# Two token batches in a transformer step: the first three tiles run ahead, and their expert rows are gathered beside the second batch

## The reference

```python
xn = rms_norm(x, norm_mix_g)
dq, dk, dv, sq, sk, sv, ga, gb = project_in(xn, w_in, pos)        # 4352 columns, RoPE on q and k
oa = diff_attn(dq, dk, dv, lam)       # 4 heads, two softmaxes each, causal by chunks of 64
ob = swa(sq, sk, sv, sinks)           # 8 heads, window of 128 tokens
h = x + (ga * (rms(oa) @ w_a) + gb * (ob @ w_b)) @ w_out
h = h + mem_attn(rms_norm(h, norm_mem_g), mk, mv, w_mem_q, w_mem_o)   # 256 memory tokens
# PEER: 128 x 128 experts of one neuron, 8 heads, each takes the best 16
q = rms_norm(h) @ w_peer_q;  s1, s2 = q1 @ keys1, q2 @ keys2
idx, g = top 16 of v1[i] + v2[j], softmax of their scores
h = h + sum over the 8 * 16 chosen of gelu(xn . u[idx]) * g * v[idx]
y = rms_norm(h, final_norm_g)
```

## Time and profile before

| | us |
|---|---|
| median of 3 runs | 4893.45 (4890.81 to 4926.24) |
| the profiled execution | 4913.51 |
| its span in the trace | 4911.7 |

### The profile page before, as it was taken

The page is one execution under the profiler, slowest core; times in us unless marked ns, Lnnn a source line. Parts: engine busy times, 40 slices in busy tenths (PEclk is TensorE's granted clock), DMA queues, the critical chain, the costliest instruction groups (busy, mean ns, idle before and its releaser), DMA issues. The chain is left out here.

```text
span 4911.7 us, 61601 instructions
## 1 busy us (share of the span) xinstructions
PE 4164.9 (85%) x20219; PEld 3480.8 (71%) x20219; DVE 3159.5 (64%) x5709; ACT 1297.4 (26%) x2699; POOL 626.9 (13%) x505
## 2 busy tenths in 40 slices
PE   6999798998887875355552699999999999999996
PEld 5788556786444665344442599999999999999996
DVE  4301333111111217999998599999999999999896
ACT  3111222111111211144443222222232223222222
POOL 0000000000000000033333111111111111111110
PEclk9999667555999977688887799999999999999998
DMA  4322320102014010022223777777777777777774
GB/s 139 112 90 77 86 65 17 41 19 86 26 34 154 0 39 5 5 73 73 73 73 96 269 278 284 285 274 281 276 287 278 277 279 274 280 276 278 273 273 173
DMA packets 323883, 770.86 MB, mean 157 GB/s; under 512 B 29120, under 2 KB 170944, under 8 KB 274112
## 3 DMA queue, kind: packets, MB, share of 16 engines
q1 hardware_dynamic: 248992, 356.77, 22.2%
q0 software_dynamic: 55360, 403.60, 21.7%
q10 hardware_dynamic: 19440, 9.44, 0.7%
HBM read 681.01 MB, written 89.78 MB: 157 GB/s over the span
## 5 line engine op out<-in xcount | busy, mean ns | idle before, releaser
L2078 PE MATMUL exp_h<-exp_xh,exp_uh 128*128 128x384 f32 x2048 | 688.8, 336 | 59.6 <-DVE exp_xl L2048 56.4
L2080 PE MATMUL exp_h<-exp_xh,exp_ul 128*128 128x384 f32 x2048 | 688.2, 336 | 0.0
L2079 PE MATMUL exp_h<-exp_xl,exp_uh 128*128 128x384 f32 x2048 | 687.4, 336 | 0.0
L1900 POOL DMA_INDIRECT exp_uv<-in_peer_uv,gidx x384 | 373.8, 973 | 1783.6 <-DVE H L2010 1735.9
L2092 PE MATMUL exp_y<-exp_vh,exp_ah 128*128 128x512 f32 x1536 | 598.2, 389 | 3.3 <-DVE H L1983 3.3
L2094 PE MATMUL exp_y<-exp_vh,exp_al 128*128 128x512 f32 x1536 | 600.6, 391 | 0.0
L2093 PE MATMUL exp_y<-exp_vl,exp_ah 128*128 128x512 f32 x1536 | 600.3, 391 | 0.0
L2004 DVE SCALAR_TENSOR_TENSOR exp_uv<-exp_uv,exp_gx 128x1024 f32<-128x1024 f32 x384 | 469.0, 1222 | 62.4 <-DMA exp_uv<-in_peer_uv,gidx 39.1
L2010 DVE SCALAR_TENSOR_TENSOR H<-exp_uv,exp_coef,H 128x1024 f32<-128x1024 f32 x384 | 491.2, 1280 | 24.0 <-ACT exp_coef L1945 24.0
L1983 DVE TENSOR_TENSOR H<-H,exp_y 128x512 f32<-128x512 f32 x768 | 490.3, 679 | 3.8 <-PE exp_y L2094 3.6
L2078 PEld LDWEIGHTS exp_h<-exp_xh,exp_uh 128*128 128x128 f32 x2048 | 386.5, 189 | 66.2 <-issue 53.6
(11 more groups left out here) (276 smaller groups left out, 6327.6 us busy)
## 6 DMA issues: line engine op xcount, KB each, us to landing
exp_u<-in_peer_u SPq DMA_DIRECT2D x128, 512.0 KB, 4.8
exp_v<-in_peer_v SPq DMA_DIRECT2D x128, 512.0 KB, 4.0
s_w<-top_tile_w SPq DMA_DIRECT2D x6, 8192.0 KB, 30.4
exp_w<-s_w SPq DMA_DIRECT2D x128, 384.0 KB, 3.0
out_z<-proj_zs SPq DMA_DIRECT2D x72, 256.0 KB, 2.0
proj_w<-in_w_in SPq DMA_DIRECT2D x16, 1024.0 KB, 5.4
merge_gates<-out_z SPq DMA_DIRECT2D x9, 1024.0 KB, 5.0
s_zt<-proj_zt ACTq DMA_DIRECT2D x27, 256.0 KB, 2.3
```

The source lines that it names most:

```text
L1900: pool.indirect_dma_start(out=uv[j][:, :], out_offset=None, in_=I["peer_uv"], in_offset=bass.IndirectOffsetOnAxis(ap=K["gidx"][:, e, j:j + ...
L2078: pe.matmul(hp[c][:, 0:TC], uh[s][:, n, :], xh[:, n, at], start=(n == 0), stop=False)
L2079: pe.matmul(hp[c][:, 0:TC], uh[s][:, n, :], xl[:, n, at], start=False, stop=False)
L2080: last = pe.matmul(hp[c][:, 0:TC], ul[s][:, n, :], xh[:, n, at], start=False, stop=(n == KD - 1))
```

## The change

- The tiles are two batches. Batch A is tiles 0 to 2, and it runs projection, both attentions, merge, memory and retrieval first. Batch B is tiles 3 to 8, and it then runs the same stages. The experts and final stages follow once for all. Every stage's weights are loaded (and, in the projection, split) in both batches. B's attention reads k and v of all tiles.
- All of A's three tiles are gathered; of B's six, two are gathered (`NG = 2`) and four dense (`ND = 4`). The output half of a dense tile is a piece; of the eight pieces five (`HELD`) stay in PSUM over all 128 steps, and three take turns in one bank `turned`, which DVE empties by `add_turn`.
- A's gathers are single rows of 4 KB (512 KB for 128 tokens): 384 of u, then 384 of v. The first 640 of them (all u, and v of tiles 0 and 1) are taken inside B's stages, by numbers in the code (`rows.take`): 110 in projection, 154 in differential attention, 120 in window attention, 120 in merge, 136 in memory. They come through a ring of four buffers (`RING`). The last 128 (v of tile 2) are taken in the experts stage, one a step (`add_early`). Two small stages are new, `phase_rows` (scales A's tiles) and `phase_coefficients` (the gelu of A's dot products).
- B's gathered tiles have two buffers each instead of one.
- In `choose` a reduction over 16 is written as four additions. Most counted loops of the first stages are unrolled.

```diff
-NG = 3
-ND = NT - NG
+NA = 3
+NG = 2
+ND = NT - NA - NG
 MD = ND * P
+RING = 4
...
+NROW = 128
+QUOTA = {"project": 110, "diff": 264, "window": 384, "merge": 504, "memory": 640}
+NU = NA * NROW
+NV_FRONT = 2 * NROW
...
+    def fetch(self, pool, stage):
+
+        K = self.K
+        end = RING if stage is None else min(QUOTA[stage] + RING, QUOTA["memory"])
+        for n in range(self.fetched, end):
+            tile, e = self.choice(n)
+            if n >= RING:
+                pool.wait_ge(K["row_used"], n - RING + 1)
+            pool.indirect_dma_start(out=K["row"][n % RING][:, :], out_offset=None,
+                                    in_=self.I["peer_u_rows"] if n < NU else self.I["peer_v_rows"],
+                                    in_offset=bass.IndirectOffsetOnAxis(ap=K["gidx"][:, e, tile:tile + 1], axis=0))\
+                .then_inc(K["row_in"][n % RING], 16)
+        self.fetched = end
...
+    def take(self, dve, count):
+        K = self.K
+        for n in range(self.taken, self.taken + count):
+            tile, e = self.choice(n)
+            row = K["row"][n % RING]
+            if n >= NU and n % 2 == 0:
+                dve.drain()
+            dve.wait_ge(K["row_in"][n % RING], 16 * (n // RING + 1))
+            if n < NU:
+                dve.scalar_tensor_tensor(out=row[:, :], in0=row[:, :], scalar=1.0, in1=K["gx"][:, tile, :],
+                                         op0=ALU.mult, op1=ALU.mult, accum_out=K["hs"][:, tile, e:e + 1]).then_inc(K["row_used"], 1)
+            else:
+                dve.scalar_tensor_tensor(out=K["H"][:, tile, :], in0=row[:, :], scalar=K["coef"][:, tile, e:e + 1],
+                                         in1=K["H"][:, tile, :], op0=ALU.mult, op1=ALU.add).then_inc(K["row_used"], 1)
+        self.taken += count
...
-        arrive = [0, 1, 2, 2, 3, 3, 4, 4, 4]
+        arrive = [0, 1, 2, 2, 3, 3][:NT]
...
-                        if t in (3, 7):
-                            low_w(c + 1, t // 7)
-                with dve.Fori(ROPED, ROPED + PLAIN - 1) as c:
+                        if rows:
+                            rows.take(dve, 2)
+                        if t in (early + 1, min(late + 1, NT - 1)):
+                            low_w(c + 1, int(t > early + 1))
+                for c in range(ROPED, ROPED + PLAIN - 1):
                     for half in range(2):
                         low_w(c + 1, half)
+                        if rows:
+                            rows.take(dve, 9)
...
                             combine(*at(pair, x - 1))
+                            if rows:
+                                rows.take(dve, 2)
...
-                with dve.Fori(1, NT - 1) as t:
+                for t in range(1, NT - 1):
+                    if rows:
+                        rows.take(dve, 9)
                     dve.drain()
                     merged(t, False)
                     normed(t + 1)
+                    if rows:
+                        rows.take(dve, 9)
                     residual(t - 1)
+                if rows:
...
-                        dve.tensor_reduce(picked[:, a, :], hot[:, :, :].rearrange("p j c -> p c j"), AXX, ALU.add)
+                        for n in (8, 4, 2):
+                            dve.tensor_tensor(hot[:, 0:n, :], hot[:, 0:n, :], hot[:, n:2 * n, :], ALU.add)
+                            dve.drain()
+                        dve.tensor_tensor(picked[:, a, :], hot[:, 0, :], hot[:, 1, :], ALU.add)
...
+PIECES = ((0, 1, 2, 3), (2, 0, 1, 3))
+HELD = {(0, 0), (1, 0), (2, 0), (0, 1), (1, 1)}
...
-        uv = [sb(f"uv{j}", [P, 2 * D]) for j in range(NG)]
+        uv = [[sb(f"uv{j}{s}", [P, 2 * D]) for s in range(2)] for j in range(NG)]
...
-        yp = [ps(f"y{x}", [P, CW]) for x in range(NY)]
+        yp = {piece: ps(f"y{piece[0]}{piece[1]}", [P, CW]) for piece in sorted(HELD)}
+        turned = ps("turns", [P, CW])
...
-                        if e:
-                            pool.wait_ge(summed, NG * (e - 1) + j + 1)
-                        n = e * NG + j
-                        pool.indirect_dma_start(out=uv[j][:, :], out_offset=None, in_=I["peer_uv"],
-                                                in_offset=bass.IndirectOffsetOnAxis(ap=K["gidx"][:, e, j:j + 1], axis=0))\
-                            .then_inc(uv_in[j], 16)
+                        if e >= 2:
+                            pool.wait_ge(summed, NG * (e - 2) + j + 1)
+                        pool.indirect_dma_start(out=uv[j][e % 2][:, :], out_offset=None, in_=I["peer_uv"],
+                                                in_offset=bass.IndirectOffsetOnAxis(ap=K["gidx2"][:, e, j:j + 1], axis=0))\
+                            .then_inc(uv_in[j][e % 2], 16)
+                    if e == 0:
+                        for _ in range(RING):
+                            rows.fetch_one(pool)
...
-                def add_up(out, half, x):
-                    dst = H[:, NG + x, half * CW:(half + 1) * CW]
-                    dve.wait_ge(y_ready, NY * (out - 1) + x + 1)
-                    dve.tensor_tensor(dst, dst, yp[x][:, :], ALU.add).then_inc(y_added, 1)
+                def add_turn(q, which):
+                    piece, half = ((3, 0), (2, 1), (3, 1))[which]
+                    dst = H[:, NA + NG + piece, half * CW:(half + 1) * CW]
+                    dve.wait_ge(turn_ready, q * 3 + which + 1)
...
+                    def add_early():
+                        row = K["row"][k % RING]
+                        dve.wait_ge(K["row_in"][k % RING], 16 * (i + k // 4 + (NU + NV_FRONT) // RING + 1))
+                        dve.scalar_tensor_tensor(out=H[:, NA - 1, :], in0=row[:, :], scalar=K["coef"][:, NA - 1, bass.ds(e, 1)],
+                                                 in1=H[:, NA - 1, :], op0=ALU.mult, op1=ALU.add).then_inc(K["row_used"], 1)
+
+                    q = i * 2 + k // 2 - 1
                     dve.drain()
+                    if k % 2 and not first:
+                        add_turn(q, 0)
+                    elif not first and not (isinstance(i, int) and i == 0 and k == 2):
+                        add_turn(q - 1, 2)
...
                         low_v(e - 1, 1 - s)
-                    dot(2)
                     dve.wait_ge(w_in[s], 16 * (i * 2 + k // 2 + 1))
                     weigh(0)
                     low_a(0)
                     weigh(1)
                     add_row(0)
                     low_a(1)
-                    if first:
-                        add_row(1)
-                        add_row(2)
-                        return
-                    add_up(e, s, 0)
-                    add_up(e, s, 1)
+                    if k % 2 and not first:
+                        add_turn(q, 1)
                     add_row(1)
-                    add_up(e, s, 2)
-                    add_up(e, s, 3)
-                    add_row(2)
-                    add_up(e, s, 4)
-                    add_up(e, s, 5)
+                    add_early()
 
...
+                    for piece in PIECES[half]:
+                        at = slice(piece * P, (piece + 1) * P)
+                        held = (piece, half) in HELD
+                        dst = yp[piece, half] if held else turned
+                        if not held:
+                            which = half + (half and piece == 3)
+                            pe.wait_ge(turn_added, q * 3 + which + 1)
                         for n in range(GROUP):
...
+        run(phase_project, K, I, S, A)
+        attend(A)
+        run(phase_memory, K, I, S, A)
+        run(phase_retrieve, K, I, S, A)
+        with ExitStack() as scope:
+            K["row"] = [keep(f"row{r}", [P, D], scope=scope) for r in range(RING)]
+            with ExitStack() as inner:
+                K["gx"] = keep("gx", [P, NA, D], scope=inner)
+                run(phase_rows, K, I, rows)
+                run(phase_project, K, I, S, B)
+                attend(B)
+            run(phase_memory, K, I, S, B)
+        run(phase_retrieve, K, I, S, B)
+        K["row"] = [keep(f"late_row{r}", [P, D]) for r in range(RING)]
+        run(phase_experts, K, I, S, rows)
+        run(phase_final, K, I, S)
```

789 lines of the change are left out of this document (487 added, 302 removed).

## The result

The changed kernel takes 4862.61 us (median of 8 runs), the one before 4902.41 in the same comparison: ratio 0.9911, 95% interval 0.9888 to 0.9934. It is 0.9% faster where 8.4% was forecast. The profiled execution took 4867.1 us against the 4497 of the sum, so 370 us are to be found.

The account below looks back on a forecast made before the run. The experts stage was taken as bound by TensorE with VectorE just behind; 4913.5 + 192 (stages run twice) - 608 (experts at 11.8 us a step) = 4497 profiled, 20 above the median, so 4480 us; range 4365 to 4700.

Parts of the forecast that it names:

- 1410: B's five stages that take rows, projection to memory: 351 + 305 + 289 + 247 + 218 us.
- With 3 us of landing it is 1.3, and nothing is added. I take the second: B's stages: a single-row gather lands in 3 us, four buffers give a row each 1.3 us, adding nothing.
- 40 us: Kept for the range if B's rows land in 5.5 us: 1.9 us a row, memory 258 instead of 218.
- 6 in 11.4 us is 275 GB/s: B's differential attention: six row gathers fit in a tile's 11.4 us, so gathers are not late.
- In a step of 16.2 us that left about 6 us over; in 11.8 it is 1.5: Experts stage: slack of u, landing in 4.8 us plus 1.1 us of ScalarE, before `low_u` needs it.
- (a): Rival, experts stage: transfers come late, u issued after `low_v`; 13 us a step, +155, 4635 us; chance 0.18.
- its 0.8 us of slack in a step covers: Experts stage: TensorE waits some 0.7 us for bank `turned`, covered by its slack in a step.
- 16.17 us: Experts stage before the change: spacing of two equal dot products, taken to match VectorE's 16.2 us sum per step.
- (d): Rival, B's stages: gathers starve, row instructions wait long; at 2.5 us a row +266, 4750 us; chance 0.04.
- the supply term: A's projection: weights arrive in two halves, 20 to 27 us a chunk; 231 us, or 193 if hidden.
- (c): Rival, experts stage: TensorE's clock falls to 1.2 GHz, step doubles to 22 us for 45 steps; 4940 us; chance 0.04.
- (b): Rival: TensorE sets the experts pace, 11.2 us a step, and 30 less in front; 4375 us; chance 0.12.

Follow-up runs that it names:

- b_dve: Changed kernel with every VectorE row instruction kept in B's stages but only the first four rows gathered; B's five stages take 1461 us without gaps.
- b_dma: Changed kernel with all 640 gathers kept in B's stages but each row instruction replaced by a one-element copy; B's five stages take 1503 us without gaps.
- b_none: Changed kernel without gathers or row instructions for the 640 rows in B's stages; B's five stages take 1310 us without gaps.
- ring5: Changed kernel with five row buffers instead of four in B's stages; 4760 us.
- u_first: Changed kernel with SyncE's waits in the experts stage in the order buffers come free, so u is issued earlier; 4712.8 us.
- no_uv: Changed kernel without the experts stage's gathers for the two gathered tiles, except the first two experts'; 4711.4 us.
- no_late: Changed kernel with only four of the experts stage's 128 late row gathers, row instructions kept; 4712.6 us.
- u_first_no_late: Changed kernel with both the reordered SyncE issues (early u) and only four late row gathers in the experts stage; 4707.7 us.

## Why the prediction was wrong

Two steps failed: the gathers in B's stages were put at nothing, and the slack of u in the experts stage was too large. B's five stages took 1659 us for 1410; 198 of the 249 us go with the gathers (b_dve has 1461), 51 with the rest.

**The gathers in B's stages.** The failed step is "With 3 us of landing it is 1.3, and nothing is added. I take the second". Bounds of 5.5 and 1.5 us stood beside it, and measured were 5.5 to 5.8. No row stood behind the 3; the nearest one, the larger gather at 5.5, was the value to take. By its formula the Trainium skill, "DMA: Bandwidth & Descriptors", in the anatomy of a DMA issued from GpSimd, gives an estimate of 3.2 us. The measurement decides against that for gathers issued behind one another beside a stage's own loads. But even the upper bound was priced too low. I kept 40 us for it, on the check that the rows of a tile fit into the tile's period, and gathers alone cost 212 us (b_dma against b_none). One buffer more gave back 107 of the changed kernel's 1693 in the five stages (ring5). In b_dma the gathers lengthen four of the five stages, memory by 81 us and differential attention by 61, though "6 in 11.4 us is 275 GB/s" had passed them there. The rows are taken in bunches of 2 to 12, of up to 19 at a stage's end, and only four are ever ahead; that this is why the check by the period failed is my reading. A part is another thing, the stages' own loads made slower: the projection's weights land in 5.7 us in b_dve, 8.7 in b_dma and 9.2 in the changed kernel. How the 212 divide between the two was not separated.

**The row instructions in B's stages.** I let 1410 us stand for B's five stages with them. Without gathers they add up to 1461. Merge was right (247, measured 246), differential attention near (305, 317), window attention too dear (289, 264), projection too cheap (351, 372, of which 358 stand even without rows). Memory was mis-sized: 218 forecast, 262 measured. Its 32 us a tile assumed a full VectorE, and VectorE is busy for 203 of the 262 us (b_dve). The two engines wait for each other: TensorE stands for `bmem_xt`, which VectorE makes between rows, for 50 us there and for 10 without rows.

**The experts stage.** The failed step is "In a step of 16.2 us that left about 6 us over; in 11.8 it is 1.5". The mechanism of rival (a) is what came: u is issued after `low_v`, lands late, and `uh` and `ul` wait. It was priced at 13 us a step and is 12.81; the stage is 127 us over the forecast. u_first shows it by taking exactly this away. The slack was computed with the landing of 4.8 us from the kernel before; with the changed kernel's gathers and loads beside it u landed in 7.2, which ate it. What the forecast did not see is that the buffer had been free for a whole step.

With everything in time 11.8 was forecast and 11.6 measured, but that is partly luck, since 11.8 was VectorE's sum and the step is TensorE's. TensorE is the fuller engine (0.98 against 0.93). Its 256-column matmuls follow each other at 120 ns (4003.99 to 4004.11 in u_first), not 116, so its own pace is 11.2 and not 11.0. And the wait for `turned`, which "its 0.8 us of slack in a step covers", is not covered, since TensorE has no slack: it adds 0.4 us a step. The 16.17 us that seemed to confirm VectorE's sum was one pair of dot products; over 108 steps of the kernel before the `low_u` instructions start 16.49 us apart.

**The rivals as alternatives.** (a) and (d) had chances of 0.18 and 0.04 as if one excluded the other. They sit in different stages and both draw on one quantity, how long a transfer takes on a busy chip. (d)'s sign, row instructions waiting for gathers, came with landings of 5.5 us, not the 9 it was thought to need to be slower than before; the ring matters as (d) says, and the bunches, which its pace leaves out, are my reading of the rest. 4480 + 155 + 266 = 4901 is what both together would have given; 4863 came. The range up to 4700 held (a) alone (4635), but neither (d) alone (4750) nor the two together, so it was too narrow at that end.

**What held.** The stages of A: projection 243 us (231; the supply term stands, well over 193), differential attention 70 (80), memory 125 (145). Retrieval took 192 + 568 + 32 for the last store = 792 (810). The share that the DMA engines would reach held too: 0.92 was forecast for a short step, and u_first has 0.92. (c) came only in small: the granted clock of the experts stage is 0.95 to 0.96, which is the 0.3 us a step above, and 1.00 once the waits are gone. (b)'s faster pace, 11.2 a step, was not reached in any run. One reading was wrong without effect on the sum: TensorE fills 84% of merge and of memory, not 86 or more.

## What to carry to other kernels

Where a queue's engine waits for several buffers in a fixed order, write the waits in the order in which the buffers come free: here one issue stood a whole step behind its freed buffer, which cost nothing at 16.5 us a step and 150 us in the shorter one. Size a ring of gathers by its round trip during the bunch in which it is drained, not by the average over the stage, and look for tiles that are dead by then and can be buffers. When a change puts more transfers beside a load, ask what a longer landing of it would do, and add up rivals that can both come true.

## What the runs showed of the hardware

A gather of the same 0.5 MB lands in 4.4 us in the experts stage, at a DMA share of 0.86, and in 5.5 to 6.3 us in B's stages at 0.75, where four to seven of them are under way at once. In the experts stage it is issued after VectorE's last instruction of a step, ahead of the uv gathers, and its landing hardly moves with the share: 4.3 us in no_uv at 0.50, 4.4 in u_first at 0.92. The share does not tell the landing of u either: 4.9 us in no_uv at 0.50, 4.8 in no_late at 0.83, 3.7 in u_first_no_late at 0.84, and 7.2 and 7.3 in the changed kernel and u_first at 0.87 and 0.92, the two with both kinds of gathers in full. What is queued with a transfer seems to tell more of its landing than the share does; no run isolates it.

GpSimd's instruction that issues a gather is not of fixed length. Its mean was 1001 ns (u rows) in b_dma, where VectorE has no row instructions, and 1265 in the changed kernel; the DMA shares of B's stages are 0.75 to 0.87 there and 0.73 to 0.79 here. For the uv gathers it was 973 ns in the kernel before, 1318 in the changed one and 1595 in u_first, but 1329 in no_late, whose step is as short as u_first's. The v rows (mean 1190 and 960) in the view of one line, changed kernel and then b_dma (min/median/max ns):

```profile
L111 POOL DMA_INDIRECT row<-in_peer_v_rows,gidx x256: 932/939/1990, 1910.9 to 2536.6; - x128
```

```profile
L111 POOL DMA_INDIRECT row<-in_peer_v_rows,gidx x256: 932/936/1928, 1818.3 to 2373.1; - x128
```

The medians of these are equal; single instructions take about twice as long, over 1500 ns in 63 of 256 in the changed kernel and in 4 of 256 in b_dma. That VectorE's long instructions hold GpSimd's up is my reading, and no run tested it.
